# Moving exponentials, squares and border work within the mixers' chunk loop of a hybrid decoder layer

## What is computed

```python
def chunked_gated_linear_attention(q, k, v, log_decay, chunk):     # GLA, HGRN
    def step(state, inp):
        b = jnp.cumsum(gi, axis=2)
        o_inter = jnp.einsum('bhcd,bhde->bhce', qi * jnp.exp(b), state)
        rel_decay = jnp.where(causal, jnp.exp(rel), 0.0)            # rel[i,j] = b[i] - b[j]
        scores = jnp.einsum('bhid,bhjd,bhijd->bhij', qi, ki, rel_decay)
        o_intra = jnp.einsum('bhij,bhje->bhie', scores, vi)
        k_to_end = ki * jnp.exp(b_last[:, :, None, :] - b)
        state = state * jnp.exp(b_last)[..., None] + jnp.einsum('bhcd,bhce->bhde', k_to_end, vi)
        return state, o_inter + o_intra

def ssd_chunked_scan(x, dt, a_neg, bm, cm, chunk):                  # SSM
    def step(state, inp):
        decay = jnp.where(causal, jnp.exp(seg), 0.0)                # seg[i,j] = b[i] - b[j]
        w = decay * cb[:, :, None] * dti[..., None, :]
        y = jnp.einsum('bgrij,bgrjp->bgrip', w, xi)
        y = y + jnp.einsum('bgin,bgrpn->bgrip', ci, state) * jnp.exp(b)[..., None]
        state = state * jnp.exp(b_last)[..., None] + ...
        return state, y
# then per branch: rms_norm, times silu(gate); y_ssm first gets + d * x and * silu(z)
# g = sigmoid(h @ w_gates): the gates of the merge
```

## Time and profile before

| | |
|---|---|
| device time, median of 3 runs | 2066.76 us (2061.98 to 2069.88) |
| the profiled execution: its time, its span | 2060.14 us, 2058.4 us |
| busy over the span: PE, DVE, ACT, POOL | 94%, 71%, 51%, 11% |
| granted PE clock, mean | 0.976 of 2.4 GHz |
| the mixers' eight chunks | about 610 to 1084 us in the span |

### The profile page before, as it was taken

One profiled execution on the slowest core, in us unless ns is written; L12 is line 12 of the kernel. 1 busy time (PEld: TensorE's weight loads), 2 busy tenths in 40 slices (PEclk: granted clock), 3 DMA queues, 4 the chain that ended last, 5 costly groups with the idle time before them and its releaser, 6 DMA issues. The chain is left out here.

```text
span 2058.4 us, 26797 instructions
## 1 busy us (share of the span) xinstructions
PE 1926.0 (94%) x10602; PEld 1576.0 (77%) x10603; DVE 1470.7 (71%) x1687; ACT 1047.2 (51%) x1234; POOL 216.7 (11%) x173
## 2 busy tenths in 40 slices
PE   6999999999999989899998999995999999999993
PEld 5789888888977767677776788874788888888882
DVE  5966467666236877878775565556898889999875
ACT  5234344444225444445444334333788888878763
POOL 3310000000020000000001000012122222222210
PEclk9999999999999999999999999997999999999997
DMA  5242333333264557645536655462999999999986
GB/s 167 85 143 72 113 103 105 121 103 110 96 160 139 147 147 173 165 114 155 161 101 260 239 192 192 178 232 100 352 374 385 388 384 387 388 390 385 388 328 257
DMA packets 212415, 436.11 MB, mean 212 GB/s; under 512 B 28018, under 2 KB 151042, under 8 KB 184770
## 3 DMA queue, kind: packets, MB, share of 16 engines
q1 hardware_dynamic: 179394, 355.68, 50.0%
q10 hardware_dynamic: 20864, 53.49, 7.4%
q0 software_dynamic: 12032, 25.22, 3.2%
HBM read 369.67 MB, written 81.43 MB: 219 GB/s over the span
## 5 line engine op out<-in xcount | busy, mean ns | idle before, releaser
L1602 PE MATMUL psum<-h_hi,l_hi 128*128 128x512 f32 x384 | 159.1, 414 | 3.3 <-PEq L58 3.3
L1602 PE MATMUL psum<-h_lo,l_hi 128*128 128x512 f32 x384 | 159.9, 416 | 0.0
L1602 PE MATMUL psum<-h_hi,l_lo 128*128 128x512 f32 x384 | 157.2, 409 | 0.0
L2741 DVE TENSOR_TENSOR gu_lo<-up_raw,gu_hi 128x2048 fp32r<-128x2048 f32 x64 | 146.2, 2286 | 13.2 <-ACT gu_hi L2684 13.2
L2684 ACT CAST gu_hi<-up_raw 128x2048 fp32r<-128x2048 f32 x64 | 122.1, 1909 | 35.0 <-PE u_ps L2813 35.0
L1258 ACT COPY l_out<-psum 128x512 f32<-128x512 f32 x48 | 28.1, 586 | 176.5 <-PE psum L1602 170.0
L2457 PE MATMUL mpsum<-y_hi,wb_hi 128*128 128x512 f32 x256 | 102.9, 402 | 11.1 <-DVE y_lo L2217 9.1
L2813 PE MATMUL g_ps<-gu_hi,xeT_hi 128*128 128x512 f32 x256 | 104.7, 409 | 5.9 <-DVE xeT_lo L2750 5.9
L806 DVE TENSOR_TENSOR w_lo<-w_raw,w_hi 128x512 fp32r<-128x512 f32 x90 | 61.8, 688 | 65.4 <-ACT w_hi L662 65.4
L662 ACT CAST w_hi<-w_raw 128x512 fp32r<-128x512 f32 x90 | 55.8, 622 | 91.8 <-PE ps L931 91.3
L2457 PE MATMUL mpsum<-y_hi,wb_lo 128*128 128x512 f32 x256 | 101.4, 396 | 0.0
(11 more groups left out here) (465 smaller groups left out, 5415.3 us busy)
## 6 DMA issues: line engine op xcount, KB each, us to landing
up_raw<-moe SPq DMA_DIRECT2D x62, 1024.0 KB, 8.1
gate_raw_a<-moe SPq DMA_DIRECT2D x33, 1024.0 KB, 8.6
gate_raw<-moe SPq DMA_DIRECT2D x33, 1024.0 KB, 8.6
dn_raw_a<-moe SPq DMA_DIRECT2D x31, 1024.0 KB, 7.3
dn_raw<-moe SPq DMA_DIRECT2D x31, 1024.0 KB, 8.1
w_raw<-w_in SPq DMA_DIRECT2D x26, 1024.0 KB, 6.0
l_raw<-w_gates ACTq DMA_DIRECT2D x24, 512.0 KB, 6.3
s_gates<-l_out ACTq DMA_DIRECT2D x48, 256.0 KB, 4.3
```

Source lines behind the costliest of these rows:

```text
L1602: ins = nc.tensor.matmul(psum[:, bank, :], w[t % 2][:, k, :], x[:, k, half * 512:half * 512 + 512], start=i == 0, stop=i == LATE_MM - 1, s ...
L2741: nc.vector.tensor_tensor(gu_lo[p][:], gu_raw[p][:], gu_hi[p][:].bitcast(F32), ALU.subtract).then_inc(gu_ready, 1)
```

## The change

ACT's and DVE's `body(c)` are reordered; no instruction is added or taken away, and PE's and SP's lists stay as they are.

- ACT: `relative(c, 4)` and `relative(c, 5)` go ahead of the SSM squares and the small exponentials (one before `late(h0)`, one after); `relative(c, 6)` ahead of the second eight SSM differences (L1308); the eighth set's exponential and that of `b_in` (L1329, L1330) ahead of `late(h0 + 2)` and of the exponential of the decay matrix (L1322).
- DVE: `scores_in(0)` and `factors(2)` go ahead of `intra_in`; `x_weighted` and `x_in_sum` go behind `factors(3)`, and the late difference `late(h0 - 1)` goes behind `z_gated`.

```diff
@@ ACT, body(c)
                 relative(c, 2)
                 relative(c, 3)
+                relative(c, 4)
                 late(h0)
+                relative(c, 5)
                 if c:
                     ssm_squares(c - 1)
                 act.wait_ge(wdarg_ready, c + 1)
...
-                relative(c, 4)
                 act.wait_ge(small_ready, c + 1)
                 differences(range(SSM_HEADS // 2))
                 late(h0 + 1)
-                relative(c, 5)
                 if c:
                     ssm_scale(c - 1)
+                relative(c, 6)
                 differences(range(SSM_HEADS // 2, SSM_HEADS))
-                relative(c, 6)
+                i = NE * c + NL
+                act.wait_ge(d_ready, i + 1)
+                nc.scalar.activation(ex[i % 3][:], ex[i % 3][:], ACT.Exp).then_inc(e_ready, 1)
+                nc.scalar.activation(b_in[b][:], b_in[b][:], ACT.Exp).then_inc(eb6_ready, 1)
                 late(h0 + 2)
                 act.wait_ge(seg_ready, SSM_HEADS * (c + 1))
                 nc.scalar.activation(wmat, wmat, ACT.Exp, scale=-1.0).then_inc(wexp_ready, 1)
...
-                i = NE * c + NL
-                act.wait_ge(d_ready, i + 1)
-                nc.scalar.activation(ex[i % 3][:], ex[i % 3][:], ACT.Exp).then_inc(e_ready, 1)
-                nc.scalar.activation(b_in[b][:], b_in[b][:], ACT.Exp).then_inc(eb6_ready, 1)
@@ DVE, body(c)
                 dec(i0 + 4)
                 if c:
                     gla_hgrn_out(c - 1)
-                    intra_in(c - 1, 1)
-                    x_weighted(c - 1)
-                    late(h0 - 1)
                 else:
                     late(3)
                 scores_in(0)
                 factors(2)
                 if c:
-                    x_in_sum(c - 1)
+                    intra_in(c - 1, 1)
                 scores_in(1)
                 dec(i0 + 5)
                 factors(3)
                 if c:
+                    x_weighted(c - 1)
+                    x_in_sum(c - 1)
                     z_gated(c - 1)
+                    late(h0 - 1)
```

## The result

| | device time, median | runs |
|---|---|---|
| before | 2064.37 us (2058.71 to 2069.88) | 4 |
| changed | 2041.81 us (2034.39 to 2042.53) | 4 |

The ratio is 0.9893, with a 95% interval of 0.9872 to 0.9915: 17.5 to 26.4 us less. In a later comparison on one chip the same kernel gave 0.9902 (0.9884 to 0.992). The change makes the kernel about 1% faster, as forecast (2047 us, range 2036 to 2058).

The account below looks back on a forecast made before the run. PE's idle time and clock were the bound: 36.6 us of waits plus 4.5 of clock falls, less 17.3 of new waits and 4.5 of new falls, saves 19.3. The median 2066.8 becomes about 2047.5, given as 2047 us, range 2036 to 2058.

Parts of the forecast that it names:

- What bounds the stage: PE in the mixers: 5.32 us of waits in chunk 2's 60.00 us; without them 54.68 us a chunk.
- Levels 2 and 3, L1710, the keys: PE's waits of 1.39 (2.44 in odd chunks), 0.87, 0.44 and 1.43 us there would all go.
- The stall that goes to `cbm`, even chunks: PE's transposes behind `cbm`, held by `wd`'s load: 2.7 us wait, so an even chunk loses 2.7 instead of about 5.3.
- ACT held in odd chunks: ACT's load waits for the moved late difference, delaying the squares: new 2.3 us wait at PE's means, L1657.
- The slow load: One decay matrix load took 18.2 us against 16.3; such a one would cost 1 to 2 us more, once.
- the fourth case of the prediction: Gain given back at the decay matrix's load: landing 2 us later takes 14 of 23.8 us, leaving 2057; chance 0.15.
- The clock: PE's clock falls after waits: three old falls, about 4.5 us, go; three of seven new waits bring 4.5 back.
- the 1.5 us that the prediction named as a bound: Sign at PE's new waits: prediction wrong if the low clock takes more than 1.5 us behind each gap.
- The argument that longer matmuls around the gaps speak against a fall: New PE waits of 2.3 to 2.7 us stand between longer matmuls, so three falls were taken, not seven.
- Chunk 0: No border work; its two waits at `cbm` and the keys, 2.4 us, go because exponentials of levels 4 to 7 come earlier.
- The sum: Over the stage: 41.1 us taken away, 17.3 of new waits and 4.5 of clock falls put in, 19.3 saved.
- D: The start of L1641 in a chunk, from which PE's, DVE's and ACT's times are counted; 723.77 in chunk 2.

Follow-up runs that it names:

- The kernel with nearly all waits gone: Changed kernel with `cbm` ahead of `wd` and the load of `late(h0)` behind the squares; 0.9769 of the kernel before, again 0.9777.
- Two kernels that release the load by different edits: Changed kernel with the late difference put back behind the scaled outputs, 0.9880 of before; or with ACT's load of `late(h0)` behind the squares, 0.9850.

## Why the prediction was right, point by point

- **What bounds the stage.** PE's list without waits was put at 54.68 us a chunk. The kernel with nearly all waits gone took 54.31. In the second profile of the changed kernel, chunk 2 took 57.10 - 3.04 = 54.06 without its wait. So PE's list is up to 0.6 us a chunk shorter than counted: in an even chunk each stretch loses 0.1 to 0.2 with its wait (from L1720 to the next D 18.35 before, 18.20 now). Why is not shown.
- **Levels 2 and 3, L1710, the keys.** All waits gone, as computed.
- **The stall that goes to `cbm`, even chunks.** Forecast 2.7; measured 2.52, 2.80 and 2.65.
- **ACT held in odd chunks.** Forecast 2.3 at the means; measured 2.39 to 2.41 in all four, with ACT idle 8.18 or 8.19 us. (The "5.2 to 5.9" that an odd chunk lost before counts a fall of the clock with the waits, and the 2.3 does not.) Two kernels that release the load by different edits removed it.
- **The slow load.** Forecast as 1 to 2 us once, but left out of the sum. In chunk 5 `wd` waited 1.99 us for the DMA and `cbm` then cost PE another 1.11. In the second profile of the changed kernel the waits in chunks 4 and 6 were 4.41 and 4.28; there `wd` waited 2.90 and 2.94 us for the load. This is what the fourth case of the prediction describes, in two chunks of seven, and it takes part of the gain in some executions.
- **The clock.** I took three falls, 4.5 us. The profile had five, in chunks 1, 2, 3, 4 and 6 (the second profile four). Counted between fixed points of PE's list, against the same stretches without a fall, they cost 1.5 to 1.7 us each, about 7.7 us. That term was undersized by 3.2 us in this execution, by the count of falls more than by their price; the price lies at the 1.5 us that the prediction named as a bound, and for the two falls at the means slightly above it. The argument that longer matmuls around the gaps speak against a fall is not borne out: over all the profiles, waits of 2.38 to 2.41 us ahead of the means were followed by one in 9 of 16 cases, those of 2.44 and 2.45 ahead of level 2 in 8 of 12. The estimate by the Trainium skill ("TensorE: Matmul & The Clock Gate", on oscillation in real kernels: half of the time at the low clock) lies at the upper end: about 3.5 us at 0.5 gives 1.7, and the rows say 1.5 to 1.7.
- **Chunk 0.** Forecast 2.4 us of gain, measured 0.8. PE came earlier to two late halves whose bank ACT had not yet evicted, 0.45 and 1.08 us; ACT's copy in turn stood behind a store that had not landed (2.59 us). I had not followed the evictions at all, since no row of before shows such a wait.
- **The sum.** 19.3 us forecast, 15.9 in the profiled execution of the stage, 22.6 between the medians. The forecast lies within the interval. It was 36.6 of waits less 17.3 of new ones, with the falls of the clock taken as three and three. Measured were 20.2 us of new waits (1.5 of them in chunk 0, 1.1 in chunk 5) and 3.2 us more for the clock, and against that 2.7 us less in PE's list. So the mechanism was right at each wait, and that the sum came so near owes something to luck: its errors partly cancel.

What the prediction did not see is that the two halves of the change are of such different worth. It worked out each wait of the whole, and it said where the stall goes, but it did not ask what each half would do alone.

## What to carry to other kernels

Before moving work out of one wait, compute where the waiting engine arrives next and what fixes that place: here a load at D + 18.4 and a product queued behind it gave back much of what the levels won, and moving one 0.7 us instruction ahead of that wait (with the held load moved too) doubled the gain, from 20.3 to 48.5 us on one chip. When an instruction is moved that only frees a buffer, look for who asks for it: a transfer that waits in an engine's list holds everything behind it, even if nobody needs the transfer soon. And test the halves of a change alone, since one can carry it all while the other waits for its obstacle to be removed.

## What the hardware showed that I had not expected

- PE's waits of 2.38 to 2.45 us in this stage were followed by the lower clock in 17 of 28 cases (ten profiles were counted), those of 2.5 to 4.7 us in 15 of 17, and those below 2.2 us only once, where 1.63 and 1.88 stood close together. The same chunk of the same kernel fell in one execution and not in the next (chunk 3 of the changed kernel, after 2.41 and 2.40 us). A fall took mostly 3 to 4 us at 1.2 GHz, in five cases about 7.
- A load of 1024 KB that repeats 16 rows of 512 bytes to all 128 partitions took 14.7 to 19.1 us, one of half its size 11.5 to 19.9, while plain loads of 1024 KB in the kernel before have medians of 6.0 to 8.6.
